# A two-block transformer kernel: another order for the front of its first block, with token scales at evictions and the output projection in two halves

## The reference, cut to what matters

```
hn = x * rsqrt(mean(x*x) + eps) * attn_norm
z = hn @ w_in                       # 1024 x 2048: q, k, v, u of 512 columns each
q, k = rope(rms_norm(q, q_norm)), rope(rms_norm(k, k_norm))     # heads of 64
w = softmax(q1 k1' / 8) - lam * softmax(q2 k2' / 8)             # 4 heads, causal
a_out = rms_norm(w @ v, subln) * (1 - lambda_init)
p_out = ((window means of u) - u) @ w_pool * pool_scale         # windows 2, 4, 8, 16
h = x + concat(a_out, p_out) @ w_out
h = h + moe(rms_norm(h, ffn_norm))  # 32 experts of 12 MB each, 4 per token
```

## Time and profile before

| what | value |
|---|---|
| median of 3 runs | 1925.64 us (1925.25 to 1929.62) |
| the profiled execution | 1930.75 us |
| its span, first to last instruction | 1929.0 us |
| TensorE busy / weight loads | 1744.8 us (90%) / 798.3 us |
| VectorE, ScalarE, GpSimd busy | 392.6, 259.3, 27.3 us |
| mean granted clock of TensorE | 0.972 of full speed |
| DMA | 667.69 MB, mean 346 GB/s |
| chain of waits | DMA 51%, PE 43%, DVE 3%, ACT 1% |

### The profile page before, as it was taken

How to read it: one execution, slowest core, us unless ns; L and a number is a source line. 1 busy time by engine, 2 the same in 40 slices (tenths; PEclk the granted TensorE clock), 3 DMA queues, 4 the chain that set the end, 5 groups by cost and what they waited for, 6 DMA issues and landing times.

```text
span 1929.0 us, 28248 instructions
## 1 busy us (share of the span) xinstructions
PE 1744.8 (90%) x12056; PEld 798.3 (41%) x12056; DVE 392.6 (20%) x943; ACT 259.3 (13%) x533; POOL 27.3 (1%) x104
## 2 busy tenths in 40 slices
PE   7788999999999999999999978999988888888887
PEld 3443333333233233333333334756455555555554
DVE  1623112111112112111111122153322111111111
ACT  1301111111111111111111112130011111111111
POOL 3010000000000000000000000000000000000000
PEclk9988999999999999999999978999988999999999
DMA  9414999999999999999999956332245999999997
GB/s 298 191 60 158 429 429 427 429 428 428 429 428 428 429 428 428 429 428 428 429 428 428 429 207 237 131 131 88 92 173 198 429 428 429 429 428 428 428 428 312
DMA packets 69694, 667.69 MB, mean 346 GB/s; under 512 B 9392, under 2 KB 11200, under 8 KB 31648
## 3 DMA queue, kind: packets, MB, share of 16 engines
q1 hardware_dynamic: 64864, 664.84, 82.8%
q10 hardware_dynamic: 4416, 1.49, 0.3%
q0 software_dynamic: 384, 0.93, 0.2%
HBM read 666.19 MB, written 1.05 MB: 346 GB/s over the span
## 4 chain that ended last, share of the span: by engine, by line
DMA 51%; PE 43%; DVE 3%; ACT 1%; issue 1%; SPq 1%; DVEq 0%; ACTq 0%
DMA ring<-in_w_up 34%; DMA ring<-in_w_up_experts 17%; PE ps L1306 13%; PE ps L1479 12%; PE ps L1333 4%; PE ps L1185 3%; PE ps L1291 2%; PE ps L1360 2%; PE ps L1254 2%; PE ps L1169 1%; PE ps L1379 1%; PE ps L1264 1%; SPq L298 1%; PE ps L1579 1%; PE ps L1316 0%
## 5 line engine op out<-in xcount | busy, mean ns | idle before, releaser
L1306 PE MATMUL ps<-ring,Z 128*64 128x512 f32 x3168 | 709.7, 599 | 36.6 <-DMA ring<-in_w_up 35.9
L1306 PEld LDWEIGHTS ps<-ring,Z 128*64 128x64 f32 x3168 | 218.7, 137 | 501.9 <-issue 416.3
L1333 PE MATMUL ps<-ring,Z 128*32 128x128 f32 x4096 | 247.4, 408 | 63.8 <-DMA ring<-in_w_gate_experts 32.8
L1333 PEld LDWEIGHTS ps<-ring,Z 128*32 128x32 f32 x4096 | 149.3, 126 | 152.8 <-DMA ring<-in_w_up_experts 44.1
L1479 PE MATMUL ps<-ring,xT 128*128 128x512 f32 (+1 forms) x384 | 163.0, 582 | 1.5 <-DVE xT L669 0.8
L882 DVE TENSOR_SCALAR Z<-ps 128x512 f32<-128x512 f32 x33 | 22.8, 692 | 440.7 <-PE ps L1306 440.7
L1291 PE MATMUL ps<-xs,Z 128*32 128x256 f32 (+1 forms) x800 | 106.1, 477 | 3.9 <-DVE Z L854 3.9
L1479 PEld LDWEIGHTS ps<-ring,xT 128*128 128x128 f32 x384 | 72.8, 192 | 83.0 <-issue 80.2
L884 DVE TENSOR_SCALAR Z<-ps 128x512 f32<-128x512 f32 x33 | 22.8, 692 | 251.0 <-PE ps L1306 251.0
L514 ACT COPY Z<-ps 128x256 f32<-128x256 f32 x65 | 24.2, 372 | 340.6 <-PE ps L1341 340.6
L523 ACT COPY Z<-ps 128x512 f32<-128x512 f32 (+1 forms) x65 | 31.2, 480 | 287.9 <-PE ps L1306 244.4
(11 more groups left out here) (335 smaller groups left out, 1132.8 us busy)
## 6 DMA issues: line engine op xcount, KB each, us to landing
ring<-in_w_gate SPq DMA_DIRECT2D x66, 2048.0 KB, 23.0
ring<-in_w_up SPq DMA_DIRECT2D x66, 2048.0 KB, 25.6
ring<-in_w_down SPq DMA_DIRECT2D x66, 2048.0 KB, 21.4
ring<-in_w_gate_experts SPq DMA_DIRECT2D x32, 2048.0 KB, 17.0
ring<-in_w_up_experts SPq DMA_DIRECT2D x32, 2048.0 KB, 21.5
ring<-in_w_down_experts SPq DMA_DIRECT2D x32, 2048.0 KB, 12.9
ring<-in_w_in SPq DMA_DIRECT2D x13, 2048.0 KB, 9.7
ring<-in_w_out SPq DMA_DIRECT2D x4, 2048.0 KB, 17.4
```

The lines of the kernel that those rows point to most:

```text
L1306: last = pe.matmul(dst[CAP * j:CAP * (j + 1)], lhsT, rhs(j), start=start, stop=True, skip_group_check=True)
L1333: last = pe.matmul(bank(4)[CAP2 * t:CAP2 * (t + 1), P * s:P * (s + 1)], picked[:, chunk * CAP2:(chunk + 1) * CAP2], v[:, c, t:512:4], star ...
```

## The change

It touches the front of the first block alone (and the semaphore counts that later parts compare with).

- The w_in parts are loaded and projected in the order k, q, u (the pool part), v.
- SP loads only the attention gain ahead of the weights. The other four gain vectors, and nine of the 18 small loads of ScalarE's queue, become 13 "late" loads on SP's queue behind w_out. VectorE waits for them ahead of the residual adds.
- TensorE transposes x itself as each tile lands. The token scale `rstd` is applied where a projection is evicted: ScalarE writes `Z` with scale=rstd, and for q and k also the squares. The eviction takes banks 0 and 1 in turn, so projection j waits for eviction j-2.
- k and q are normed and turned one after the other, k while q is projected.
- TensorE's order: six projections (k, q, u); transposes of q and k; pool window products; scores; projection 6 (v, tile 0); pool output; projection 7; transposes of the attention weights, with those of the pool half of the mix between them; a quarter of the output projection (`out_half(0, 1)`, the pool half's four chunks of block 0); attention times v; the other three pool quarters; transposes of the attention half; the four attention quarters.
- w_out is loaded with chunk c holding rows 128c to 128c+127, and not every eighth row.

The core of the diff (left out are the changes in indices, numberings and bank numbers):

```diff
@@ sync
-            for k, name in enumerate(("attn_norm", "ffn_norm", "ple_gate_norm", "norm1_w_2", "norm2_w_2")):
-                sp.dma_start(gcol[:, k, :], w[name][0].rearrange("(p c) -> p c", p=P)).then_inc(sem("gains_loaded"), 16)
+            sp.dma_start(gcol[:, A_NORM, :], w["attn_norm"][0].rearrange("(p c) -> p c", p=P)).then_inc(sem("gain_loaded"), 16)
             for s, (src, c, n) in enumerate(front):
                 sp.dma_start(slot(s, c, n), src).then_inc(full[s], 16)
+            for k, name in enumerate(("ffn_norm", "ple_gate_norm", "norm1_w_2", "norm2_w_2")):
+                late(gcol[:, k + 1, :], w[name][0].rearrange("(p c) -> p c", p=P))
+            for k, name in enumerate(("q_norm_w_2", "k_norm_w_2")):
+                late(qkw2[:, k, :], w[name][0].partition_broadcast(P))
...
+            late(hnorm[:, :], w["hgrn_norm_w_2"][0].partition_broadcast(P))
@@ scalar
+            def leave_z(j):
+                part, a = PARTS[j // 2], j % 2
+                act.wait_ge(sem("proj"), j + 1)
+                act.wait_ge(sem("rstd"), 1)
+                if part in (Q, K):
+                    act.activation(sq[:, a, 512 * part:512 * (part + 1)], bank(j % 2), ACT.Square, scale=rstd[:, a:a + 1])\
+                        .then_inc(sem("squares"), 1)
+                lo = PART_LO[part]
+                act.activation(Z[:, a, lo:lo + 512], bank(j % 2), ACT.Identity, scale=rstd[:, a:a + 1]).then_inc(sem("z_copied"), 1)
+            for j in range(2):
+                leave_z(j)
+            act.wait_ge(sem("mean_sq"), QK_NTH[0])
+            act.activation(qrt[:, 16:32], qms[:, 16:32], ACT.Sqrt).then_inc(sem("root"), 1)
             act.wait_ge(sem("angles"), 1)
             act.activation(trig[:, :, :, :], red[:, :, :, :], ACT.Sin).then_inc(sem("trig"), 1)
...
+            leave_z(6)
             act.wait_ge(sem("row_max"), 2)
...
+            leave_z(7)
@@ vector
-            norm(A_NORM)
+            for b in range(4):
+                a, half = b // 2, b % 2
+                dve.wait_ge(sem("norm_turned"), b + 1)
+                tt(xT[:, 4 * half:4 * half + 4, a * P:(a + 1) * P], bank(4 + b).rearrange("p (c t) -> p c t", c=4),
+                   gcol[:, A_NORM, 4 * half:4 * half + 4, None].broadcast_to([P, 4, P]), ALU.mult)\
+                    .then_inc(sem("norm_xT"), 1)
...
+            for nth, part in zip(QK_NTH, (K, Q)):
+                dve.wait_ge(sem("squares"), 2 * (nth - 1))
+                step(dve.tensor_reduce(sums_qk[:, part], sq[:, :, 512 * part:512 * (part + 1)].rearrange("p a (g d) -> p a g d", d=64), X, ALU.add))
...
+                rope(v, 0, 8)
...
+            dve.wait_ge(sem("late_loaded"), 16 * N_LATE)
             for b in range(4):
...
@@ tensor
+            for b in range(4):
+                pe.wait_ge(sem(f"x_loaded{b // 2}"), 16)
+                turn(bank(4 + b), h[:, b // 2, :], 4 * (b % 2), DC, 4, "norm_turned")
+            def project_in(j):
+                u, a = j // 2, j % 2
+                pe.wait_ge(sem("norm_xT"), 2 * a + 2)
+                pe.wait_ge(full[u], 16)
+                if j >= 2:
+                    pe.wait_ge(sem("z_copied"), j - 1)
...
+            for j in range(6):
+                project_in(j)
+            pe.wait_ge(sem("roped"), 2)
...
+            project_in(6)
+            pe.wait_ge(sem("row_max"), 1)
...
+            project_in(7)
...
+            turn_w(0, 0, 0, 6)
+            pe.wait_ge(sem("mix_ready"), TT)
+            for a in range(TT):
+                turn_chunks(bank(2 + a), xs[:, a, 512:1024])
+            pe.wait_ge(sem("w_copied_dve"), 1)
+            turn_w(1, 1, 0, 7)
+            turn_w(2, 1, 1, 6)
+            pe.wait_ge(sem("mix_copied_act"), 2)
+            pe.wait_ge(sem("z_copied"), 8)
+            out_half(0, 1)
...
+            for b in range(1, 4):
+                out_half(b, 1)
+            pe.wait_ge(sem("mix_ready"), 2 * TT)
+            for a in range(TT):
+                turn_chunks(bank(6 + a), xs[:, a, 0:512])
+            for b in range(4):
...
+                out_half(b, 0).then_inc(sem("out1"), 1)
```

More of the change, by code:

```diff
@@ L151, in cols @@
             return src[:, :, lo:lo + n], src.shape[1], n
-        front = [cols("w_in", 512 * k, 512) for k in range(4)] + [cols("w_out", 512 * k, 512) for k in range(2)]
+        PARTS = (K, Q, U, V)
+        PART_LO = {Q: 0, K: 512, V: 1024, U: 1536}
+        front = [cols("w_in", PART_LO[part], 512) for part in PARTS]
+        front += [(w["w_out"][0].rearrange("(c p) n -> p c n", p=P)[:, :, 512 * k:512 * (k + 1)], DC, 512) for k in range(2)]
         def slot(s, c, n):
@@ L724, in _ @@
             step(ts(subln[:, :], subln[:, :], 1.0 - LAMBDA_INIT, None, ALU.mult))
[L726 to L735, removed]
-                step(tt(qk[:, a], qk[:, a], qrs[:, 16 * a:16 * a + 16, None].broadcast_to([P, 16, 64]), ALU.mult))
-                for k in range(2):
-                    v = qk[:, a, 8 * k:8 * k + 8, :]
-                    step(tt(v, v, qkw[:, k, None, :].broadcast_to([P, 8, 64]), ALU.mult))
-            rope(qk, 0, 16)
             for a in range(TT):
@@ L796, in _ @@
                 v = h[:, a, 512 * n:512 * n + 512]
-                tt(v, bank((5, 6, 7, 0)[b]), v, ALU.add).then_inc(sem("residual"), 1)
+                tt(v, bank((4, 5, 0, 1)[b]), v, ALU.add).then_inc(sem("residual"), 1)
             def experts(k):
@@ new lines, in out_half @@
+            def out_half(b, half):
+                n, a = b // 2, b % 2
+                pe.wait_ge(full[4 + n], 16)
+                for c in range(4 * half, 4 * half + 4):
+                    last = pe.matmul(bank((4, 5, 0, 1)[b]), xT[:, c, a * P:(a + 1) * P], slot(4 + n, DC, 512)[:, c, :],
+                                     start=c == 4, stop=c == 3)
+                return last
+            turn_w(0, 0, 0, 6)
+            pe.wait_ge(sem("mix_ready"), TT)
+            for a in range(TT):
+                turn_chunks(bank(2 + a), xs[:, a, 512:1024])
@@ L1248, in _ @@
-            pe.wait_ge(sem("mix_copied_dve"), 2)
-            pe.wait_ge(sem("mix_copied_act"), 2)
-            for b in range(4):
-                n, a = b // 2, b % 2
-                pe.wait_ge(full[4 + n], 16)
-                for c in range(DC):
-                    last = pe.matmul(bank((5, 6, 7, 0)[b]), xT[:, c, a * P:(a + 1) * P], slot(4 + n, DC, 512)[:, c, :],
-                                     start=c == 0, stop=c == DC - 1)
-                last.then_inc(sem("out1"), 1)
+            for b in range(1, 4):
+                out_half(b, 1)
```

167 lines of the change are left out of this document (94 added, 73 removed).

## The result

| | before | after |
|---|---|---|
| median | 1925.45 us (4 runs, 1924.94 to 1929.62) | 1899.03 us (4 runs, 1895.69 to 1901.66) |
| profiled execution, span | 1930.75, 1929.0 us | 1897.65, 1895.9 us |
| mean granted clock | 0.972 | 0.983 |

The ratio of the runs is 0.9853, with a 95% interval of 0.9836 to 0.9869: 28.3 us faster, between 25.2 and 31.6 (the two medians themselves lie 26.4 apart). The forecast was 30.3 faster, 1895.3, in a range of 1888 to 1906. The gain is 1.5% of the time, and the whole interval lies beyond the 5.8 us that the prediction took as the least that can be told from no change.

What follows compares the result with a forecast made beforehand. The front delays the second expert's loads, which start a DMA-full stream, so it counts one for one. Start 2.7, idle 21.6 and clock 7.0, less 1.0 of new waits, make 30.3: 1925.6 to 1895.3 us, range 1888 to 1906.

Steps and rivals of the forecast that it cites:

- That the front counts one for one: First block's front: ending it earlier moves the second expert's first SP load, and everything behind, by the same amount.
- Start: Up to the first input projection: w_in's first load lands 1.9 sooner, projections start at 12.0, 2.7 us sooner (0.9 to 6.1).
- The loss before the full pace: First input projections: 2.7 us lost before TensorE reaches full pace, left as it is.
- Projections: Six input projections (k, q, u) before attention, done at 55.9; evictions and the norms of k and q cost TensorE nothing.
- The tight place: ScalarE's third eviction, behind k's root and the sine, done near 38.5; projection 4 wants it at 42.2.
- The rival that priced late small loads: Input projections: w_pool lands at 48.2 and projection 4 waits 10.4, giving 1905.8; chance 0.06.
- Attention and output: Scores to the last attention quarter: v and pool work cover softmax and head norm; idle 9.27, 4.31 and 6.64 goes; ends 114.0.
- new waits: Waits the new order adds in attention and output, 1.0 us taken off the gain.
- Half clock: Front's TensorE work: with no idle over about 1 us the clock should hold, saving 7.0 us.
- The rival of a falling clock: Transposes and waits at 80 to 82 and 98.7 to 100 drop the clock, 2.3 each, giving 1899.9; chance 0.07.
- Moved loads: Thirteen late loads on SP's queue behind w_out: at 2 us per issue they land by 80 and cost nothing.
- the slower rival: Late loads crawl on SP's queue and hold the residual adds: plus 29.5, 1955.1; chance 0.03.

Runs made afterwards that it cites:

- v_first: The change with all eight input projections, v included, ahead of attention; 1911.34 us median, ratio to before 0.9913.
- out_whole: The change with the output projection in one piece per block behind the attention; 1908.52 us, ratio to before 0.9908.
- quarters: The change with w_in's first load cut in four, and k's and q's norm waiting only for their gains' loads; 1892.40 us, ratio 0.9823.
- small_back: The change with nine small loads back on ScalarE's queue, k's norm waiting for all 18; 1915.92 us, one run.

## Why the prediction was right

*That the front counts one for one.* Right, within some 4 us. The chain was argued from SP's load at 178.56. It moved by 29.85 with a front of 29.96, and in v_first and out_whole, which make the front longer by 16.5 and 10.0, the load moved by 18.9 and 9.7 and the medians by 12.3 and 9.5. The 3.1 by which the profiled span fell more than the front, and the 3.5 by which the medians fell less, are of the size by which equal code scatters behind the front: 1743.5 to 1750.4 for the rest, 26.6 to 30.2 for the router. No run here shows it more finely: by the medians v_first gives back 12.3 for 16.5, out_whole 9.5 for 10.0, quarters gains 6.6 for 6.7.

*Start.* The one step with a wrong size. The prediction let w_in's first load land 1.9 sooner because it is issued 1.9 sooner. It was issued at 2.17, but took 10.8 instead of 9.7, and the first projection began at 13.07, not 12.0: 1.7 gained, not 2.7, and with 1.5 us of scatter around it. That x was still moving is a likely reason for the longer landing, but no run tests it, and it is within the scatter. The lower bound, 0.9, was nearer. The loss before the full pace was 43.50 - 41.2 = 2.3, taken as 2.7. Quarters shows what the term could have been: its projections start at 8.44, next to the prediction's earliest bound of 8.6, and lose 0.2.

*Projections.* Right: six in one row, gapless, done at 56.4 (55.9 predicted). k was ready at 42.5 and q at 50.4, against 41 and 51. The tight place, the third eviction, was done at 40.45, and projection 4 was due near 42.8. w_pool landed at 36.0 and not 34: it was issued at 15.83 and not near 20, but took 20.2 and not 14.0. That half of ScalarE's loads had to go has no term in the prediction; small_back shows that it carries 15 us, by the time that ScalarE is held issuing them. The rival that priced late small loads had 10.4, by the landing, and the wrong projection.

*Attention and output.* Right within a few tenths: scores end at 64.5 (64.4), v's second half at 80.15 (80.0), last weights ready at 80.5 (80.4 to 81.4), attention times v ends at 88.6 (88.4), the last pool quarter at 98.9 (98.7), the mix ready at 95.3 (95.7), the end at 114.3 (114.0). Of 1.0 us of new waits 0.35 showed.

*Half clock.* Right: no fall in the front, from the clock's first record at 17.2 on. The rival of a falling clock did not happen. The clock held at 1.00 through the turns at 80 and 99. By the rule of the Trainium skill ("TensorE: Matmul & The Clock Gate", "Part 4: PE-mode transpose"), under which transposes do not count as busy work in the same way, these were idle stretches of about 2.3 and 1.0 us, and no run here shows whether longer ones would bring the clock down. At the start, traces of this case go against the rule. In quarters TensorE's only work ahead of the projections is the 16 turns of x, and the projections run at the full pace at once. In the change run again the first record of the clock, at 1.00, stands at 8.2, behind the same 16 turns; the clock falls while TensorE waits for the weights and comes back at 18.4:

```profile
8.50:11.90 3.40, 0.00 (x0) 0.00 (x0) 0.63 (x2) 0.20 (x1) 3.08 (x12) 0.96 1.04 392
11.90:18.70 6.80, 5.87 (x8) 2.53 (x9) 0.00 (x0) 0.00 (x0) 5.97 (x27) 0.52 1.00 320
```

In the change and in the kernel before the same turns were not enough: there the full pace comes only at 17.2 and 19.7, some way into the projections. What decides between the two is open.

*Moved loads.* They took 16.6 us to issue (32.84 to 49.46), 1.3 each on average, half of it the first (8.11), below the 2 taken and far below the 7.1 at which the slower rival decides. The first residual add waited for TensorE, not for them.

*The sum.* Start 1.7, waits 21.6, clock 7.0 + 0.4, less 0.35 is 30.3, and 29.96 was measured. Most of the 0.4 between them may lie in the clock's term: it takes the 16 turns of 110.01 as 1.8 at the full pace, and in the change they take 2 x 1.04. The forecast's 30.3 has the same total, but with 1.0 too much in its first term, and 0.6 too much of new waits and 0.4 too little of clock against it: that they cancel is luck. One sum in the prediction is off: the low end of the forecast's own range, 1889, is 1890.5 by its own terms (3.4 and half of 2.7 below 1895.3). Nothing hangs on it.

## What to carry to other kernels

Find the first event behind a stage that releases a saturated transfer stream; if it moves with the stage, the stage is worth its time one for one (here within some 4 us), however small its share of the span. Cover for another engine's chain is best bought with independent dense work that is needed anyway (here a projection and half of another), and it pays twice, in idle time and in the clock behind it. When a start moves forward, ask at once what it now waits for: here a 2 MB load that, cut in four, let the projections start 4.6 us sooner and at the full pace.

## What was not expected of the hardware

- A 2 MB load issued at 2.17 behind x lands at times that scatter by 1.5 us between executions (first projections at 12.83 to 14.30 in six executions with the same loads; 15.01 in small_back, whose ScalarE issues more loads meanwhile).
- The granted clock can fall during a run of narrow matmuls (128x32) that keeps TensorE busy by the profile (behind 123 in 120.95 to 126.1 of the change), also with four dense ones just ahead of the norm. Where it falls moves equal stretches by up to 3.6 us (26.58 to 30.20), though the spans of the change's two profiled executions differ by only 1.0.
- The clock can rise behind transposes alone: in quarters the six projections take 41.44 behind the 16 turns of x, with no slow start, and 43.1 to 44.2 in the runs where TensorE waits for weights in between.
- A queue that issues loads can hold its engine for a long time: ScalarE was held from 9.0 to 41.8 by 20 small loads, 7.38 of it by one of 64 KB.
